# Constant products ahead of five waits of TensorE, in a recurrent decoder step on one core

## The reference

```
mod = silu(c) @ w_ada + b_ada                      # six vectors: sh1, sc1, g1, sh2, sc2, g2
h   = rmsnorm(x, g_norm1) * (1 + sc1) + sh1
proj = h @ w_in                                    # inputs of three parallel head groups
o_hg = hgrn2(q, k, v, logf)                        # 4 heads, matrix state 64 x 64
y_mb = ssd(x, dt, A, B, C)                         # Mamba-2, 8 heads, 2 groups, state 64
o_rw = rwkv7(r, w, k, v, kk, a)                    # 4 heads, state 64 x 64
x   = x + g1 * (concat(o_hg, y_mb, o_rw) @ w_out)
h   = rmsnorm(x, g_norm2) * (1 + sc2) + sh2
x   = x + g2 * ((silu(h @ w_gate) * (h @ w_up)) @ w_down)     # D_FF = 2816
y   = rmsnorm(x, g_final)
```

## Time and profile before

| | |
|---|---|
| median of 3 runs | 1986.81 us (1985.63 to 1986.86) |
| profiled execution | 1994.82 us, span 1993.1 us |
| mean granted clock of TensorE | 0.89 |
| TensorE matmul busy | 1673.1 us (84%) |
| VectorE busy | 978.0 us (49%) |
| ScalarE busy | 589.7 us (30%) |
| GpSimd busy | 254.5 us (13%) |

### The profile page before, as it was taken

One profiled execution on the slowest core, in us unless ns is written; L12 is line 12 of the kernel. 1 busy time (PEld: TensorE's weight loads), 2 busy tenths in 40 slices (PEclk: granted clock), 3 DMA queues, 4 the chain that ended last, 5 costly groups with the idle time before them and its releaser, 6 DMA issues.

```text
span 1993.1 us, 32180 instructions
## 1 busy us (share of the span) xinstructions
PE 1673.1 (84%) x13599; PEld 1519.4 (76%) x13599; DVE 978.0 (49%) x2112; ACT 589.7 (30%) x1055; POOL 254.5 (13%) x333
## 2 busy tenths in 40 slices
PE   4898888887988627587788877999979999999995
PEld 2898777876877513256677777988869999999995
DVE  5405436665543346766666734555553333433334
ACT  2214223312422233123433434433342212222222
POOL 3500001110100032012233331000000000000000
PEclk9899889888987758568888999999989999999998
DMA  8110001010100055242221233433312131222311
GB/s 298 37 53 22 22 16 39 29 40 26 58 30 29 8 170 162 75 146 73 61 62 54 69 118 88 121 101 107 118 56 82 56 96 56 76 84 61 92 47 54
DMA packets 199302, 149.23 MB, mean 75 GB/s; under 512 B 6479, under 2 KB 187200, under 8 KB 198136
## 3 DMA queue, kind: packets, MB, share of 16 engines
q1 hardware_dynamic: 188482, 120.67, 20.1%
q0 software_dynamic: 7728, 23.27, 3.4%
q10 hardware_dynamic: 2950, 3.24, 0.5%
HBM read 134.03 MB, written 13.18 MB: 74 GB/s over the span
## 4 chain that ended last, share of the span: by engine, by line
PE 69%; DVE 19%; ACT 6%; issue 3%; DMA 2%; POOL 0%; SPq 0%; POOLq 0%; DVEq 0%; ACTq 0%
PE bank L1241 17%; PE bank L1242 17%; PE bank L1243 17%; PE bank L1180 2%; PE bank L1593 1%; PE bank L1592 1%; PE bank L1428 1%; ACT WHI L1765 1%; PE bank L1429 1%; PE bank L1377 1%; PE bank L1384 1%; PE bank L1439 1%; PE bank L1386 1%; PE bank L1524 1%; ACT PS L1993 1%
## 5 line engine op out<-in xcount | busy, mean ns | idle before, releaser
L1241 PE MATMUL bank<-HBH,WHI 128*128 128x328 f32 (+1 forms) x832 | 262.8, 316 | 14.8 <-DVE HBL L2321 10.1
L2204 DVE TENSOR_TENSOR WLO<-RAW,WHI 128x1024 fp32r<-128x1024 f32 (+4 forms) x149 | 152.1, 1023 | 238.4 <-ACT WHI L1765 237.9
L1765 ACT CAST WHI<-RAW 128x1024 fp32r<-128x1024 f32 (+4 forms) x210 | 188.0, 898 | 254.3 <-PE bank L1243 243.9
L1242 PE MATMUL bank<-HBL,WHI 128*128 128x328 f32 (+1 forms) x832 | 261.1, 314 | 0.0
L1243 PE MATMUL bank<-HBH,WLO 128*128 128x328 f32 (+1 forms) x832 | 260.1, 313 | 0.0
L1241 PE MATMUL bank<-HHI,WHI 128*128 128x344 f32 x624 | 215.6, 345 | 11.8 <-DVE HLO L2417 6.5
L1242 PE MATMUL bank<-HLO,WHI 128*128 128x344 f32 x624 | 207.3, 332 | 0.0
L1243 PE MATMUL bank<-HHI,WLO 128*128 128x344 f32 x624 | 206.6, 331 | 0.0
L1002 POOL TENSOR_TENSOR WLO<-RAW,WHI 128x1024 fp32r<-128x1024 f32 (+1 forms) x61 | 131.1, 2152 | 506.3 <-ACT WHI L1765 506.2
L1241 PEld LDWEIGHTS bank<-HBH,WHI 128*128 128x128 f32 x832 | 158.6, 191 | 16.5 <-issue 16.3
L1243 PEld LDWEIGHTS bank<-HBH,WLO 128*128 128x128 f32 x832 | 158.7, 191 | 0.0
(11 more groups left out here) (554 smaller groups left out, 3157.5 us busy)
## 6 DMA issues: line engine op xcount, KB each, us to landing
RAW<-in_w_gate SPq DMA_DIRECT2D x44, 512.0 KB, 3.9
RAW<-in_w_up SPq DMA_DIRECT2D x44, 512.0 KB, 3.9
RAW<-in_w_ada SPq DMA_DIRECT2D x32, 512.0 KB, 4.2
RAW<-in_w_in SPq DMA_DIRECT2D x26, 512.0 KB, 3.8
ADAW<-in_w_ada SPq DMA_DIRECT2D x8, 1024.0 KB, 19.9
RAW<-in_w_out SPq DMA_DIRECT2D x16, 512.0 KB, 4.3
RAW<-in_w_down SPq DMA_DIRECT2D x32, 256.0 KB, 2.7
RAW<-in_w_down SPq DMA_DIRECT2D x16, 384.0 KB, 3.5
```

Of the source, the lines that this page charges most:

```text
L1241: mm(bank[:, 0:w], whi[:, k, :], hi_k, start=(k == 0), stop=False)
L1242: mm(bank[:, 0:w], whi[:, k, :], lo_k, start=False, stop=False)
L1765: a.copy(w_split(i)[0][:, 0:nk, :], RAW[u % NRAW][:, 0:nk, :]).then_inc(w_hi, 1)
L2204: v.tensor_tensor(wlo[:, 0:nk, :], RAW[u % NRAW][:, 0:nk, :], whi[:, 0:nk, :].bitcast(F32), ALU.subtract).then_inc(w_lo, 1)
```

## The change

In blocks 0, 1 and 2 TensorE multiplies two constants, `headsum` and `triu`, into the first 128 columns of bank 7, several times, ahead of five waits: `att` and `S` in `hg_o`, and `seg`, `L` and `m` in `mb_prod`. The waits for `seg` and `L` in `mb_prod` are new, and stand in all blocks. From block 3 on `beat` does nothing.

```diff
@@ -1484,6 +1484,12 @@
             M0, M1, M2 = BK8[4:7]
 
+            def beat(b, n):
+
+                if b < 3:
+                    for _ in range(n):
+                        mm(BK8[7][:, 0:P], headsum[:, :], triu[:, :], start=True, stop=True)
+
             def pre():
@@ -1533,7 +1539,9 @@
                 elif stage == 'o':
+                    beat(b, 6)
                     pe.wait_ge(*V('att'))
+                    beat(b, 6)
                     pe.wait_ge(*V('S'))
@@ -1582,6 +1590,11 @@
                 elif stage == 'prod':
+                    beat(b, 6)
+                    pe.wait_ge(*V('seg'))
+                    beat(b, 8)
+                    pe.wait_ge(*A('L'))
+                    beat(b, 6)
                     pe.wait_ge(*V('m'))
                     pe.wait_ge(mb_pool, step(MB_POOL, 'ce', b))
```

## The result

The changed kernel takes 2000.83 us (median of 4, 1998.57 to 2002.66) against 1986.84 before; the ratio is 1.0067, interval [1.0051, 1.0083]. Timed once more beside before on another chip it took 2000.16 against 1988.04, ratio 1.0059 [1.0038, 1.0080]. So it is 12 to 14 us slower. I forecast 6.0 us slower, 1992.8 in a range to 1999: the sign was right, the size was half of it, and the cause of the rest was not among my rivals.

The account below looks back on a forecast made before the run. TensorE was taken as the bound, with low-clock `prod` on the path in blocks 0 to 2. Block terms 1.2 + 2.9 + 1.6 plus 0.3 for instructions gave +6.0 us on 1986.81: 1992.8, range 1985 to 1999.

Parts of the forecast that it names:

- the term "Instructions": TensorE's fetch of 384 more instructions: 0.3 us slower, taken between bounds 0 and 1.7 from its stalls put down to issue.
- The path: Blocks 0 to 2: VectorE stands idle for `prod`, 9.01, 10.51 and 6.66 us, so the end of `prod` is on the path.
- Clock: Added products bring `prod` of blocks 0 to 2 to full clock, 5.90 us; won 3.7, 4.1 and 3.3, 11.1 in all.
- The rival that the clock is not kept: `prod` stays at low clock, the 11.1 us are not won: +21 us, 2008, or 1998 for one block; chance 0.10.
- Price of a product: Each added product costs 0.255 us at full clock and 0.464 at 0.5, as L1581 does; the weight load sets it.
- 79p - 14.2: All terms together in us, p being a product's price at full clock, same mix in block 1; zero at p = 0.18.
- The rival by which a load is saved: An unchanged stationary costs no load: p = 0.115, sum -5.1 us, 1981.7, faster; chance 0.07.
- that by which part of it hides: A load runs partly under the pass before: p 0.13 to 0.23, sum within 4 us of nothing, 1987 at 0.18; chance 0.06.
- Block 0: Added products start `prod` 4.9 us late and end it 1.2 late; VectorE's later slack is 1.93; the 1.2 passes on.
- Block 1: 12 products vanish in the wait before `hg_o`; 20 bare before `prod` cost 7.0, less 4.1 won: 2.9 us late.
- Block 2: 1.7 us left from `hg_o`, 20 products 5.1 less 0.37 idle, less 3.3 won: 3.1 late, 1.6 after two VectorE waits.
- the gain reaches further: Rival: full clock outlasts `prod`, shortening L1581 in block 2 and `att` in blocks 2 and 3: +0.9, 1987.7; chance 0.12.

Follow-up runs that it names:

- Two pairs of kernels that differ by 128 instructions of ballast: Change, and change with products shrunk to 32x32 by 32 columns, each without and with 32 tiny products ahead of the phase: +12.1 and +14.0 against +4.2; +14.4 against +2.3 us.
- the ballast of 96 alone: Kernel before with 96 tiny products (32x32 by 32 columns) at the start of the second phase, none in the blocks: +5.5 us, ratio 1.0026.
- the kernel with 40 products in the wait: Kernel before with full-size products, 8 ahead of sm2 (block 0), 40 ahead of sh6 (block 1), plus tiny ballast: 1981.03 against 1988.19 us, ratio 0.9961.
- the tiny version: The change with each product shrunk to 32x32 by 32 columns, same places and number of instructions: +14.4 us on before, ratio 1.0080.
- with the borders of block 1 kept, the change: The changed kernel with 32 tiny products more at the start of the second phase: +4.2 us on before, ratio 1.0006 [0.9989, 1.0023].
- the second trace of before: The kernel before, unchanged, timed and traced again: 1988.12 against 1987.26, ratio 1.0000; the traced execution took 1984.64 us.
- those of 64: Kernel before with 64 tiny products (256 instructions) at the start of the second phase: -0.5 us, ratio 0.9990.
- the change with 32: The changed kernel with 32 tiny products (128 instructions) more at the start of the second phase: +4.2 us on before, ratio 1.0006.
- the tiny version with 32: The change with products shrunk to 32x32 by 32 columns, plus 32 tiny ones ahead of the phase: +2.3 us on before, ratio 1.0013.
- 54 products in three waits: Kernel before with full-size products, 8 ahead of sm2 (block 0), 40 of sh6 (block 1), 6 of sm8 (block 2), plus tiny ballast: 1976.84 against 1988.19 us, ratio 0.9927.

## Why the prediction was half of the change

**The step that failed is the term "Instructions"**, 0.3 us "between the bounds 0 and 1.7". I had seen stalls put down to issue and priced them by their number and longest size. They are not a price per instruction. TensorE crosses a border of its instruction transfers every 256 instructions; in `att` it runs through 384 in 1.8 to 2.4 us where nothing stops it, faster than they come, and stands. What the stall costs depends on where it falls. In the kernel before, the border in block 1 lies behind the last product of `att`: VectorE's HAS is already released, and the stall is 1.2 and 1.8 us in its two traces, in an ada product. The 32 products of block 0 move it into `att`, where HAS waits for all of it, and it is longer there, 4.0 to 5.1 us in each of the six traces that have it there. Two pairs of kernels that differ by 128 instructions of ballast put it at 8 to 10 us (12.1 and 14.0 less 4.2) and at 12 (14.4 less 2.3), the ballast of 96 alone at 5.5; these kernels were timed on different chips, each beside the kernel before. My rivals held everything fixed but the products' own price and clock; none moved the code.

Step by step:

- *The path:* right. `prod` at full clock comes out at VectorE's YS. It is 4.1 us shorter in blocks 0 and 1 of the kernel with 40 products in the wait, and YS is 4.1 and 4.6 us sooner after HAS there.
- *Clock:* right, with its price. 5.9 us at 1.00 in three blocks, 11.1 us won. The rival that the clock is not kept is refuted; its counterpart, the tiny version, shows what that looks like.
- *The rule of the Trainium skill ("TensorE: Matmul & The Clock Gate", Part 1) that a busy TensorE is let up to full clock:* the trace disagrees once more, 10.00 us busy at 0.50 in the tiny version.
- *Price of a product:* slightly high. 20 took 4.63 and 4.73 us, not 5.1; 12 took 2.94, not 3.1. In block 1 the 20 took 5.69, not 7.0: fewer ran at the low clock. That makes p 0.23 to 0.245, and by 79p - 14.2 the sum +4.1 to +5.2. The rival by which a load is saved, p = 0.115, is refuted; that by which part of it hides gave p from 0.13 to 0.23, and the price lies at or over its upper edge.
- *Block 0:* `prod` began 4.1 us late by the earlier trace rows (3.4, and this trace ran 0.7 ahead at HAS of block 0) against 4.9, and its end was 0.4 late, or even by the second trace, against 1.2. The slack of 1.93 us at XD took nothing: it is 0.42 us in the change and in the second trace of before alike.
- *Block 1:* +1.2 from HAS to YS, forecast 2.9. The wait ahead of `hg_o` is 5.08, near the 4 I gave.
- *Block 2:* forecast 1.6 after the waits, 3.1 at YS; measured -0.3 at YS in the first trace of the change and +1.6 in its second. In the first, L1589 (before, L1581) ran in 2.05 us at full clock instead of 3.71: part of "the gain reaches further", which I gave 0.12. In the second it took 3.19, so that gain does not come in every execution.
- *Sum without borders:* with the borders of block 1 kept, the change is +4.2 us, its ratio within 0.9989 and 1.0023, so -2.2 to +4.6 us. My +5.7 lay above that: the errors of price, block 0, block 1 and block 2 all went to one side, and the 14.0 us measured at first are in spite of them. (This kernel has a long gap in block 2, so the own cost is rather less than 4.2.)
- *"In the profiled execution"*: I added the sum to a median on the strength of one trace that lay 8 us above it. The 2000.8 us that came of it is the measured median, 2000.83, by accident: the profiled execution of the change took 1998.57. The spread of single executions, 19 us, should have been in the range.
- *The signs of being wrong that I named:* none of the three came. The clock was 1.00 in each `prod`, a product cost over 0.18 us, and HAS of block 3 came 6.3 us later than in the first trace of before (9.0 by the second). All three look at the products and their clock, and none at the border.

Left open: the table's rows add up to 6.7 us of the 13.4 between the two spans; 0.7 lie before block 0. Block 3, up to its YS, adds 1.6; there the gap in `att` is 2.35 us in the change and 1.45 in the second trace of before. Another 2.8 us are between the YS of block 3 and the HAS of block 4, and 1.5 behind that. These rows, of the second trace of before and of the change, show it (22.4 us against 25.3):

```profile
934.38 1.12 DVE L2807 SCALAR_TENSOR_TENSOR YS<-XB,PAR,bank 128x128 f32<-128x128 f32 x4 [11.50 <-PE bank L1593]
956.80 1.02 DVE L2768 TENSOR_TENSOR HAS<-bank,HMK 128x384 f32<-128x384 f32 x2 [1.84 <-PE bank L1524]
```

```profile
943.46 1.12 DVE L2820 SCALAR_TENSOR_TENSOR YS<-XB,PAR,bank 128x128 f32<-128x128 f32 x4 [11.58 <-PE bank L1606]
968.72 1.02 DVE L2781 TENSOR_TENSOR HAS<-bank,HMK 128x384 f32<-128x384 f32 x2 [4.71 <-PE bank L1530]
```

The first trace of before has 25.1 us there, and the other traces of all kernels 24.0 to 27.1: the 22.4 of the second trace of before is the odd one, so this is not of the change.

Open too is what else the ballast takes away, beyond the one gap. In the four traces that have the gap at the same place (two of the change, the tiny version, 96 tiny ones) it is 25.5 to 26.1 us from YS of block 0 to HAS of block 1, and 20.1 to 21.2 in the two of before and those of 64, of the change with 32 and of the tiny version with 32. That is some 5 of the 8 to 12 us. Later code has a share: YS of block 6 to YS of block 7 is 52.8 to 54.5 us in the four and 49.7 to 49.9 in the five. But from YS of block 1 to the end the four take 1162.9 to 1168.3 us and the five 1157.1 to 1165.1, which overlap, so the sum of it is not shown.

## What to carry to other kernels

In this kernel, work that only warms the clock paid in a wait that it fits into and fills to its end or nearly so, and not in front of work that is ready. Here 54 products in three waits, with the borders of blocks 1 and 2 kept, took 11 us off; 96 in the path put 12 to 14 on, 8 to 10 of them by the moved border. Whoever adds or removes instructions of TensorE moves every later border of its instruction transfers: look for gaps put down to issue, count in whole and half transfers from the edit to the next dense stream of short instructions, and test an edit with ballast of the same number of instructions before believing what its own work costs. And compare with more than one trace where single executions spread wider than the effect.

## What the runs showed of the hardware that was not expected

- A gap inside a stream of short passes that moves by 32 passes for each 64 instructions added ahead (11, 43, 75 passes before the end of `att`), repeats after 256, and lasts 4.0 to 5.1 us in block 1. It ends 1.20 to 1.58 us after a packet of 16384 bytes of the instruction queue has landed, as do all 67 stalls of this kind in the 16 traces. The Trainium skill ("Runtime: NRT & Kernel Launch", Instruction fetch mechanics) has the 256 right; "mostly hidden" is not what a stream of 384 instructions in about 2 us shows.
- `prod` ran for 10.00 us without a gap at 0.50 and did not come up, and it ran for 5.90 us at 1.00 and did not fall. In block 1 of the change the clock came up within the 5.69 us of the 20 added products before it.
- Where TensorE stood idle for 1.86 or 4.68 us between the added products and the end of the wait, `prod` of block 1 had a mean of 0.53 and 0.50; with products to the end of the wait it had 1.00. In blocks 0 and 2, 8 and 6 products in waits of 2.45 and 1.4 us were enough for 1.00.
